# First projection, second pass: a row block's second column half is scaled one unit ahead, and its transposes stand at the beginning of a unit

## What is computed

```
def rmsnorm(x, g):
    y = xf * lax.rsqrt(jnp.mean(xf * xf, axis=-1, keepdims=True) + RMS_EPS)
    return y * g

h = rmsnorm(x, norm_mix_pre[l])                  # 512 x 1024
proj = jnp.einsum("bsd,dn->bsn", h, w_in)        # w_in is 1024 x 5128
q, k, v, f_logit, g_b, g_c, hc, gate_conv, gate_attn = jnp.split(proj, _SPLITS, axis=-1)
...                                              # v: 512 x 512, the first product that is made
```

## Time and profile before

| | before |
|---|---|
| median of 3 runs | 1313.55 us (1313.33 to 1314.04) |
| the profiled execution | 1313.93 us, of which the span from first to last instruction is 1312.1 us |
| mean granted clock of TensorE over the span | 0.999 |
| busy: PE, DVE, ACT, POOL | 1297.1, 794.8, 613.1, 298.3 us |

### The profile page before, as it was taken

One profiled execution on the slowest core, in us unless ns is written; L12 is line 12 of the kernel. 1 busy time (PEld: TensorE's weight loads), 2 busy tenths in 40 slices (PEclk: granted clock), 3 DMA queues, 4 the chain that ended last, 5 costly groups with the idle time before them and its releaser, 6 DMA issues.

```text
span 1312.1 us, 18344 instructions
## 1 busy us (share of the span) xinstructions
PE 1297.1 (99%) x7158; PEld 1084.9 (83%) x7158; DVE 794.8 (61%) x1577; ACT 613.1 (47%) x1300; POOL 298.3 (23%) x203
## 2 busy tenths in 40 slices
PE   8999999999999999999999999999999999999999
PEld 6778888888889999998887887888788878887787
DVE  4425664333479887887333647576767667677743
ACT  4335654333435444445223445555556555656531
POOL 2022310000055556540001412131222223131010
PEclk9999999999999999999999999999999999999999
DMA  6322232332533234243236322222222222223511
GB/s 229 105 57 73 57 96 65 97 96 96 204 118 111 85 127 121 73 130 112 73 104 209 113 65 67 94 73 72 80 80 95 77 73 73 74 72 133 196 33 65
DMA packets 110297, 130.35 MB, mean 99 GB/s; under 512 B 7553, under 2 KB 87425, under 8 KB 110210
## 3 DMA queue, kind: packets, MB, share of 16 engines
q1 hardware_dynamic: 104450, 112.39, 26.6%
q10 hardware_dynamic: 5760, 16.78, 3.6%
HBM read 119.72 MB, written 9.44 MB: 98 GB/s over the span
## 4 chain that ended last, share of the span: by engine, by line
PE 86%; DVE 6%; issue 4%; ACT 2%; POOL 1%; DMA 0%; ACTq 0%; DVEq 0%; POOLq 0%
PE ps L845 14%; PE ps L847 14%; PE ps L846 13%; PE ps L850 7%; PE ps L852 6%; PE ps L851 6%; PE ps L1069 5%; PE ps L1072 5%; PE ps L1071 5%; PE ps L1127 2%; DVE wlo L1506 1%; PE ps L1137 1%; PE ps L1109 1%; PE ps L1161 1%; PE ps L973 1%
## 5 line engine op out<-in xcount | busy, mean ns | idle before, releaser
L1506 DVE TENSOR_TENSOR wlo<-raw,whi 128x512 fp32r<-128x512 f32 (+1 forms) x294 | 232.8, 818 | 186.0 <-ACT whi L1191 185.3
L1191 ACT ACTIVATE whi<-raw 128x512 fp32r<-128x512 f32 (+2 forms) x338 | 208.7, 650 | 118.6 <-PE ps L847 87.7
L845 PE MATMUL ps<-whi,hth 128*128 128x512 f32 x592 | 244.2, 413 | 0.1
L847 PE MATMUL ps<-wlo,hth 128*128 128x512 f32 x592 | 231.4, 391 | 0.0
L846 PE MATMUL ps<-whi,htl 128*128 128x512 f32 x592 | 231.1, 390 | 0.0
L1926 POOL TENSOR_TENSOR wlo<-raw,whi 128x384 fp32r<-128x384 f32 (+1 forms) x44 | 49.4, 1140 | 428.2 <-ACT whi L1191 428.2
L845 PEld LDWEIGHTS ps<-whi,hth 128*128 128x128 f32 x592 | 111.3, 188 | 32.6 <-issue 9.2
L847 PEld LDWEIGHTS ps<-wlo,hth 128*128 128x128 f32 x592 | 111.1, 188 | 24.7
L846 PEld LDWEIGHTS ps<-whi,htl 128*128 128x128 f32 x592 | 111.6, 189 | 18.6
L1456 ACT ACTIVATE px<-px,nm 128x128 f32<-128x128 f32 (+3 forms) x128 | 70.7, 554 | 90.4 <-DVE nm L1839 87.1
L850 PE MATMUL ps<-hth,whi 128*128 128x512 f32 (+1 forms) x288 | 112.0, 389 | 0.0
(11 more groups left out here) (347 smaller groups left out, 2860.4 us busy)
## 6 DMA issues: line engine op xcount, KB each, us to landing
raw<-in_l_w_in SPq DMA_DIRECT2D x64, 512.0 KB, 4.7
raw<-in_w_gate_up SPq DMA_DIRECT2D x44, 512.0 KB, 4.8
raw<-in_w_in SPq DMA_DIRECT2D x13, 1024.0 KB, 5.3
raw<-in_w_down SPq DMA_DIRECT2D x10, 1024.0 KB, 5.1
raw<-in_l_w_out SPq DMA_DIRECT2D x8, 1024.0 KB, 5.2
raw<-in_w_in SPq DMA_DIRECT2D x26, 256.0 KB, 3.7
raw<-in_w_branch SPq DMA_DIRECT2D x8, 512.0 KB, 4.2
raw<-in_w_out SPq DMA_DIRECT2D x4, 1024.0 KB, 5.1
```

The source lines that it names most:

```text
L845: e.matmul(o, ah, wh[:, cs], start=a, stop=False)
L847: m = e.matmul(o, ah, wl[:, cs], start=False, stop=z)
L1191: return e.activation(out, in_, ACT.Copy, **how)
L1506: return e.tensor_tensor(out, src, hi_part.bitcast(F32), ALU.subtract)
```

## The change

Three lines move. In the first pass's last unit (`tb` 3) `scaled 1 1` is put behind `h0 1 0`. In the second pass `h0 1 tb+1` stands at the beginning of unit `v 1 tb`, no longer in its middle, and behind it `scaled 1 tb+2`, for the block after the next. Nothing is added or taken away: the same four scalings, four sets of transposes and all other instructions are issued, in another order.

```diff
                 else:
                     put("h0", 1, 0)
+                    put("scaled", 1, 1)
                     self.split(1, 4)
...
         for tb in range(TB):
             v = self.unit(1, 16, 4, "v", 1, tb)
             if tb < 3:
-                put("scaled", 1, tb + 1)
-                next(v)
                 put("h0", 1, tb + 1)
+            if tb < 2:
+                put("scaled", 1, tb + 2)
             finish(v)
             put("vo", tb)
             self.split(2, tb + 1)
```

## The result

| | before | with the change |
|---|---|---|
| median of 20 runs each | 1313.91 us (1312.68 to 1315.88) | 1311.10 us (1310.17 to 1314.56) |
| the profiled execution: time, span | 1313.93, 1312.1 us | 1310.79, 1309.0 us |
| mean granted clock over the span | 0.999 | 1.000 |

The ratio is 0.9980 with a 95% interval of 0.9974 to 0.9986. The medians differ by 2.81 us, 0.21%: a gain clear of no change. It is just past the 0.2% that the prediction named as its bound, and the interval reaches to both sides of that bound.

A forecast was written before the change was run, and what follows sets the result against it. PE, busy 99% of the span, bounds the kernel; 3.9 us of old waits less 0.67 (handover), 0.25 (third transposes) and some 0.1 (slower first matmuls) is 2.87, kept as 2.8: 1313.55 - 2.8 = 1310.7 us, range 1309.7 to 1312.0.

The forecast's parts named there:

- the 0.2% that the prediction named as its bound: Whole kernel: 0.2% (2.6 us) is about what a measurement can tell from no change; bound for faster 1310.9 us.
- fall of the clock: At 422 to 426 us, costing 1.7 us: gone gives 1309.0 (chance 0.06), one more gives 1312.4 (0.04).
- the walk: PE's stream from the first pass's last matmul to q's first, summed from old start-to-start distances: 2.87 us gained.
- Handover: Between the passes: PE waits 0.84 us, from 24.24 to 25.08, for block 1's scaling; a loss.
- 2. and 3.: Units `v 1 0` and `v 1 1`: weights' low parts hidden, block 2's transposes without wait; each 0.5 us to spare.
- step 2: Unit `v 1 0`: weights' low parts done by 26.2, second half begins at 26.7, 0.5 us to spare; next slot 28.33.
- The tight place: Block 3's transposes before `v 1 2`: scaling behind `vl`, `yal`, `htl` on DVE; transposes at 31.78, PE waits 0.25 us.
- the sum by starts: DVE's second-pass instructions spaced by traced starts (0.60 to 0.61 us): gain 2.87, kept as 2.8 us, 1310.7 us.
- the one in which each waits for the end before it: DVE instructions spaced by shown lengths (0.69 us): block 1's scaling 0.08 later, block 3's another 0.24; gain 2.5 us, 1311.0.
- 5.: Unit `v 1 3`: `htl` of block 3 releases PE at 34.32, before 35.03; no wait, q starts at 37.79.
- The gain given back behind the pass: Behind the second pass, a wait on a transfer or ACT's splits takes up to all: 1312 to 1313.5; chance 0.08.
- The slower rival: Second pass, at the 0.84 us handover wait: TensorE falls to 1.2 GHz, up to 1319.1 us; chance 0.03.

The follow-up runs named there:

- the repeat: The changed kernel run once more with no edit against the changed kernel: median 1311.57 us, ratio to before 0.9977.
- The experiment on the handover alone: Against the changed kernel, only block 1's second scaling moved further ahead, directly behind block 0's: median 1310.72 us, ratio to before 0.9976.
- both kernels with that wait: Against the kernel before, scalings unmoved: all second-pass transposes at the front of their units (1319.97 us), or block 1's alone (1316.19 us).
- the faster experiments: Against the changed kernel: block 1's scaling further ahead (1310.72 us), all scalings one step further (1309.36 us), or first pass reordered too (1309.59 us).

## Why the prediction was right

The predicted difference was 2.8 us and 2.81 were measured. That the medians agree this closely is in part luck: in the repeat they differed by 2.4, since the share of executions with a fall of the clock moves them, and within one clock by 3.0 and 3.2. The distance in the profile does not hang on that, and it was 2.90 and 2.89 us where the walk had 2.87. The time of 1311.1 lies 0.4 above the 1310.7, because the median of before, with more runs, is 1313.91 and not the 1313.55 that I started from. By its steps, with 1.19 us added for the late beginning of the profiled execution:

1. Handover: 25.08 + 1.19 = 26.27 predicted, 26.28 measured. This loss was sized right: 0.84 us by the slots, shown as 0.70 of idle time on PE, since a matmul is shown longer than its slot. The experiment on the handover alone took it away and won 0.92.
2. and 3. The low parts of the weights hid, and the transposes of gpost waited for nothing: 28.33 + 1.19 = 29.52 predicted, 29.53 measured. (One figure of step 2 is off: by its own steps the unit's seventh matmul starts at 25.80 + 5 x 0.23 = 26.95, not 26.7, so the slack was 0.7 us.)
4. The tight place: 31.78 + 1.19 = 32.97 predicted and measured. DVE's starts are 0.60 to 0.61 apart (30.36, 30.97, 31.57, 32.17) although `htl` is shown 0.69 long. Thus the sum by starts held, and the one in which each waits for the end before it, 2.5 us, did not. The page that the prediction names for that second sum does not ask for it either: in the same section, "The DRAIN you can't avoid" of "VectorE: DVE Perf Modes" in the Trainium skill, it adds that a next operation that is not held (made to wait for it) starts earlier, and these starts agree with that.
5. `v 1 3` waited for nothing; q's start 37.79 + 1.19 = 38.98 predicted, 38.95 measured.

The gain given back behind the pass did not come: the equation of spans with the second profile closes within 0.1 us. All nine profiles say the same. From q's first matmul to the end of the span it is 1269.9 to 1270.1 us in the five without a fall in the feed-forward part and 1271.3 to 1271.4 in the four with one, whatever was done ahead of q. So the time behind q's start did not change with what was won or lost ahead of it, and one fall there costs 1.4 us, where the prediction had 1.7.

Three things were missed or left unsaid. The first and the third did not move the number; the second moves medians, and is why 2.81 is in part luck:
- The prediction took the change as one. The experiments split it: the scalings' place makes 2.84 of the 2.90 us, and the transposes' place, alone, costs 6 us (falls of the clock included), and with the scalings ahead nothing either way (22.85 against 22.80 us). That the chain from transposes to `htl` is too long for six matmuls is true, but by 0.3 us per unit only, once the scaling is out of it.
- The fall of the clock was put down as a property of the kernel which might be lost or doubled, 0.06 and 0.04. It is a property of the execution: 12 of 35 runs of before and 14 of 31 of the changed kernel have a mean clock of 0.999. In the profiled executions of before and of the repeat the fall lies behind the idle time of some 2 us in the feed-forward part; for the runs without a profile its place is inferred. It moves the median of any few runs by up to 1.5 us, which is more than the uncertainty that I gave the medians.
- The slower rival needed an idle time long enough to bring the clock down; I argued only that the longest wait gets shorter. In the profiles no fall was seen behind the handover's 0.70 us of PE's idle time, nor behind the waits of up to 1.3 us elsewhere; behind 1.88 us there was one in both kernels with that wait, and behind 2.67 us one too, but behind 2.68 us in the same execution none. What decides in this range stays open.

## What to carry to other kernels

When two engines hand a small piece back and forth in front of a third, first take the step with no recent input (here a scaling of data that has long been there) out of the chain and put it where its engine idles. Where the rest of the chain stands within the unit may then not matter. Walk the new order with start-to-start distances of the old trace; in the changed kernel that gave each start within 0.03 us, and in the faster experiments the sum within 0.15 us. Such a walk does not hold a fall of the clock: for the transposes alone it gave 3.8 us of 6.95. Measure the effect between two events of the profile behind and ahead of the change, and compare times only within one mean clock: spans of single executions differed by 1.8 us for a late transfer and 1.5 us for a fall of the clock, each about half as much as the change brought or more.

## What the runs showed of the hardware that I had not expected

- The same program with the same idle time (about 2 us of PE without a matmul, at 417 to 421 us) fell to 0.53 and 0.62 of the clock for four microseconds in one execution and stayed at 1.00 in another. Of the nine profiled executions, which all have this idle time (2.05 to 2.20 us), four show a fall behind it and five do not. "TensorE: Matmul & The Clock Gate" of the Trainium skill, section "Why this matters for your kernels", advises against long PE-idle gaps between bursts of matmuls, since they bring the clock down. The traces agree in part: gaps of 1.88 to 2.67 us were followed by a fall, though not each time, and one of 2.68 us was not.
- The transfers of x at the very beginning landed at different times from one execution to the next: ACT's square of block 1, which waits for them, started at 6.59 us (before), 7.85 (the change) and 8.51 (the repeat), and the transposes of block 2 came 1.19 and 1.82 us later than before.
